# Index scores in rounds of one width, C's scores two blocks at a time, and x loaded in two column pieces

## What is computed

```python
for l in range(DEPTH):                       # DEPTH = 2
    h = _rmsnorm(x, norm_g[l])
    p = _split(h @ w_in[l])                  # 19 projections out of one
    o_a = _mla(...)                          # A: latent attention
    o_b = _diff_attn(...)                    # B: differential attention, 2 maps of 32 a head
    o_c = _dsa(p["c_q"], p["c_k"], p["c_v"], p["c_qidx"], p["c_kidx"], p["c_widx"], rel_bias, topk)
    o_d = _short_conv(...)                   # D: convolution of width 3
    y = concat([o_a * silu(p["a_gate"]), o_b * silu(...), o_c * silu(...), o_d * silu(...)])
    x = x + y @ w_out[l]
x = _rmsnorm(x, final_g)
# second_block: FFN, mixed attention, cross attention, FFN, norm
```

## Time and profile before

| | |
|---|---|
| median of 3 runs | 1757.62 us (1757.21 to 1757.74) |
| profiled execution, its own time | 1759.74 us |
| its span, first to last instruction | 1757.9 us |
| busy in the span: PE, DVE, ACT, POOL | 100%, 59%, 43%, 24% |
| chain that ended last | PE 99%, of it L1113 80% |
| weight casts L1876 on ACT (whi) | x279, 1059 ns each |
| low parts L839 on POOL (wlo) | x160, 1369 ns each |

### The profile page before, as it was taken

How to read it: one execution, slowest core, us unless ns; L and a number is a source line. 1 busy time by engine, 2 the same in 40 slices (tenths; PEclk the granted TensorE clock), 3 DMA queues, 4 the chain that set the end, 5 groups by cost and what they waited for, 6 DMA issues and landing times.

```text
span 1757.9 us, 25383 instructions
## 1 busy us (share of the span) xinstructions
PE 1749.2 (100%) x9298; PEld 1435.9 (82%) x9298; DVE 1032.4 (59%) x2170; ACT 757.8 (43%) x1396; POOL 421.5 (24%) x326
## 2 busy tenths in 40 slices
PE   9999999999999999999999999999999999999998
PEld 7778878777887888888888888889888888888887
DVE  4888776688877665555433455445756655555333
ACT  6466644546564523233233455556434322222222
POOL 4545553454644500000000332330200200000000
PEclk9999999999999999999999999999999999999999
DMA  6432123323212343333333422223322333333332
GB/s 192 129 100 73 49 65 93 96 68 105 73 49 73 103 132 96 98 96 98 102 108 103 155 61 84 85 84 109 96 73 61 91 100 97 95 95 95 102 103 94
DMA packets 54421, 166.18 MB, mean 95 GB/s; under 512 B 10200, under 2 KB 10712, under 8 KB 54328
## 3 DMA queue, kind: packets, MB, share of 16 engines
q1 hardware_dynamic: 53032, 162.12, 30.6%
q10 hardware_dynamic: 1296, 2.84, 0.5%
HBM read 162.25 MB, written 2.17 MB: 94 GB/s over the span
## 4 chain that ended last, share of the span: by engine, by line
PE 99%; DMA 0%; DVE 0%; ACT 0%; ACTq 0%; POOL 0%; issue 0%; DVEq 0%
PE proj L1113 80%; PE turned L1427 2%; PE o L1449 2%; PE proj L1591 1%; PE proj L1584 1%; PE o L1692 1%; PE o L1792 1%; PE score L1397 1%; PE turned L1079 1%; PE turned L1671 1%; PE score L1781 1%; PE proj L1301 1%; PE turned L1654 1%; PE score L1386 1%; PE score L1654 0%; PE score L1269 0%
## 5 line engine op out<-in xcount | busy, mean ns | idle before, releaser
L1113 PE MATMUL proj<-hhi,whi 128*128 128x512 f32 x1456 | 582.6, 400 | 0.0
L1113 PE MATMUL proj<-hhi,wlo 128*128 128x512 f32 x1456 | 568.4, 390 | 0.0
L1113 PE MATMUL proj<-hlo,whi 128*128 128x512 f32 x1456 | 567.4, 390 | 0.0
L1876 ACT ACTIVATE whi<-ring 128x1024 fp32r<-128x1024 f32 x279 | 295.4, 1059 | 623.7 <-PE proj L1113 602.3
L2384 DVE TENSOR_TENSOR wlo<-ring,whi 128x1024 fp32r<-128x1024 f32 x199 | 243.2, 1222 | 161.2 <-ACT whi L1876 160.7
L1113 PEld LDWEIGHTS proj<-hhi,whi 128*128 128x128 f32 x1456 | 274.0, 188 | 63.6 <-issue 10.4
L1113 PEld LDWEIGHTS proj<-hhi,wlo 128*128 128x128 f32 x1456 | 273.4, 188 | 58.6
L1113 PEld LDWEIGHTS proj<-hlo,whi 128*128 128x128 f32 x1456 | 274.1, 188 | 53.5 <-issue 0.7
L839 POOL TENSOR_TENSOR wlo<-ring,whi 128x512 fp32r<-128x512 f32 x160 | 215.5, 1369 | 339.9 <-ACT whi L1876 339.9
L857 POOL TENSOR_TENSOR prob<-prob 128x512 f32<-128x512 f32 x36 | 56.9, 1581 | 872.2 <-ACT prob L1872 872.2
L1902 ACT ACTIVATE prob<-prob,negmax 128x256 f32<-128x256 f32 (+3 forms) x208 | 114.0, 550 | 74.1 <-DVE negmax L2457 73.4
(11 more groups left out here) (379 smaller groups left out, 2436.9 us busy)
## 6 DMA issues: line engine op xcount, KB each, us to landing
ring<-wstream SPq DMA_DIRECT2D x285, 512.0 KB, 3.6
arena<-lines SPq DMA_DIRECT2D x28, 256.0 KB, 5.7
arena<-x ACTq DMA_DIRECT2D x4, 512.0 KB, 6.3
out<-arena SPq DMA_DIRECT2D x8, 256.0 KB, 2.9
arena<-mem SPq DMA_DIRECT2D x1, 1024.0 KB, 8.5
ring<-wstream SPq DMA_DIRECT2D x12, 64.0 KB, 2.2
ring<-wstream ACTq DMA_DIRECT2D x2, 256.0 KB, 7.7
arena<-rope SPq DMA_DIRECT2D x4, 128.0 KB, 6.4
```

What stands on the lines that cost most here:

```text
L1113: mm = pe.matmul(b, rounded(w), rounded(rhs(v, k)), start=(first and n == 0 and p == 0), stop=(last and n == len(blocks) - 1 and p == 2))
L1876: act.activation(rounded(dst), src, ACT.Copy, scale=scale).then_inc(ready, 1)
```

## The change

Three parts, none of which changes what is computed.

1. **Setup.** x comes in two column pieces of 512 columns, each in four transfers of 256 KB, on the queues of SyncE and ScalarE; half of the first weights stand between the pieces. The order of the column blocks is 1, 2, 3, 0, 4 to 7. TensorE issues 8 warming matmuls, the first piece's 16 transposes, 4 more small matmuls, and the first four high products, and then turns one token tile of the second piece ahead of each of the four low products. Squares are taken in halves, the second weights' rounded copy is made by GpSimd instead of ScalarE, and a copy of x moves from ScalarE to VectorE. `norm_spread` of the second job goes behind its last block.
2. **Index rounds.** `idx_unit` gives the eight units of 512 columns first, then the eight of 384, then the eight of 256. So a round has one width, and successive sums on VectorE go into the same row: a sum waits for the one just before.
3. **C.** Blocks go in the order 0, 2, 3, 1. Steps 24 and 28 issue the scores of their own 128-wide block and of the next step's 384-wide block, which share a bank (128 + 384 = 512 columns); steps 25 and 29 issue none. `attention_cost` is adapted, and `fill_plan` then gives steps 24 to 33 chunks of 4, 4, 5, 7, 4, 8, 4, 7, 5, 8 instead of 5, 3, 5, 6, 6, 6, 6, 6, 6, 7.

```diff
-WARM = 12
-X_ORDER = (1, 2, 3, 4, 5, 6, 7, 0)
+WARM = 8
+X_ORDER = (1, 2, 3, 0, 4, 5, 6, 7)
...
+C_ORDER = (0, 2, 3, 1)
 def step_qb(s):
-    return QB_ORDER[s // 2 % 4 if s < B_STEPS else s % 4]
+    return C_ORDER[s % 4] if s >= C_STEP else QB_ORDER[s // 2 % 4 if s < B_STEPS else s % 4]
...
+def double_step(s):
+    return C_STEP <= s < STEPS and s % 4 == 0
+def after_double(s):
+    return C_STEP <= s < STEPS and s % 4 == 1
...
-    elif s < 2 or B_STEPS <= s < STEPS:
+    elif double_step(s):
+        blocks += 0.25 * (step_qb(s) + 1) + 0.2 * (step_qb(s + 1) + 1)
+    elif (s < 2 or B_STEPS <= s < STEPS) and not after_double(s):
...
 def idx_unit(n):
-    return 4 * (n // (4 * (NQB - 1))) + n % 4, n % (NQB - 1) + 1
+    return n % 8, NQB - 1 - n // 8
...
         def score_bank(s, b):
+            if after_double(s):
+                return score[b][:, width(step_qb(s - 1)):S]
...
+            sp.dma_start(ident[:, :], ident_in).then_inc(ident_loaded, 16)
+            for tok in (0, 2):
+                load_x(sp, 0, tok)
+            load_w0(0, w0_loaded)
+            for tok in (0, 2):
+                load_x(sp, 1, tok)
+            load_w0(1, wload[0])
+            sp.dma_start(ring[:, 1, :], wstream[TAKE_FROM[1]]).then_inc(wload[1], 16)
...
+                for n in range(NT):
+                    high_product(n)
                 for n in range(KC + LOW_LAG):
                     if n < KC:
                         k = X_ORDER[n]
+                        if n < NT:
+                            turn_x(1, n)
+                        else:
+                            high_product(n)
                         pe.wait_ge(h_ready, n + 1)
...
-                    if k == KC - 2:
-                        pe.wait_ge(xt_out, 1)
+                    if k == KC:
+                        pe.wait_ge(xt_out2, 1)
                         norm_spread(R_NORM)
...
-                        for p, (q_part, k_part) in enumerate(((q_hi, k_hi), (q_hi, k_lo), (q_lo, k_hi))):
-                            for b in range(2):
-                                parts(b, q_part, k_part, p == 0, p == 2)
+                        for t in (s, s + 1) if double_step(s) else (s,):
+                            for p, (q_part, k_part) in enumerate(((q_hi, k_hi), (q_hi, k_lo), (q_lo, k_hi))):
+                                for b in range(2):
+                                    parts(t, b, q_part, k_part, p == 0, p == 2)
...
-            act.wait_ge(wload[1], 16)
-            act.wait_ge(hi_ready, 1)
-            make_high(1, 1)
-            act.wait_ge(h_ready, 1)
-            act.activation(xT[:, 1, :], x_bank[1][:, :], ACT.Copy).then_inc(x1_out, 1)
-            square_x(3)
+            for tok in range(NT):
+                square_x(tok, 1)
+            act.wait_ge(hi_ready, 2)
...
-                        if n < NQB - 1:
+                        if h == 0:
                             dve.tensor_scalar(index[:, qb - 1, 0:W], relu[:, n % 4, 0:W], w, None, ALU.mult).then_inc(idx_added, 1)
                         else:
-                            dve.wait_ge(idx_added, L * IDX_UNITS + (n - 2))
+                            dve.wait_ge(idx_added, L * IDX_UNITS + n)
                             dve.scalar_tensor_tensor(index[:, qb - 1, 0:W], relu[:, n % 4, 0:W], w, index[:, qb - 1, 0:W],
                                                      ALU.mult, ALU.add).then_inc(idx_added, 1)
...
-                    scores_there(L * LAYER_SM + (2 * s + 2), L * LAYER_GR + groups_before(s - 1) if s >= 2 else None)
+                    scores_there(L * LAYER_SM + (2 * s + (4 if double_step(s) else 2)), L * LAYER_GR + groups_before(s - 1) if s >= 2 else None)
```

More of the change, by code:

```diff
@@ L407, in layer_units @@
 def layer_units():
-    return [(branch, pair, qb, h, m) for branch in "BAC" for pair in range(2) for qb in QB_ORDER for h in range(2)
+    return [(branch, pair, qb, h, m) for branch in "BAC" for pair in range(2)
+            for qb in (C_ORDER if branch == "C" else QB_ORDER) for h in range(2)
             for m in range(2 if branch == "B" else 1)]
@@ L554, in build @@
         part_done = sem("part_done")
-        x_loaded = [sem(f"x_loaded{t}") for t in range(NT)]
+        x_loaded = [[sem(f"x_loaded{i}_{t}") for t in range(NT)] for i in range(2)]
+        sq_split = sem("sq_split")
         ident_loaded, gain_loaded, par_loaded = sem("ident_loaded"), sem("gain_loaded"), sem("par_loaded")
@@ L878, in _ @@
                     .then_inc((w0_lo, lo_ready)[half], 1)
+            pool.wait_ge(wload[1], 16)
+            for half in range(2):
+                cols = slice(half * SLOT // 2, (half + 1) * SLOT // 2)
+                last_copy = pool.tensor_copy(rounded(whi[:, 1, cols]), ring[:, 1, cols])
+            last_copy.then_inc(hi_ready, 1)
             pool.wait_ge(hi_ready, 2)
@@ L1064, in _, with turn_x @@
             pe.wait_ge(ident_loaded, 16)
-            for tok in range(NT):
-                pe.wait_ge(x_loaded[tok], 16)
-                for c in range(KC):
+            def turn_x(piece, tok):
+                pe.wait_ge(x_loaded[piece][tok], 16)
+                for c in range(4 * piece, 4 * piece + 4):
+                    if c == KC - 1 and tok == 0:
+                        pe.wait_ge(x0_out, 1)
                     mm = pe.transpose(x_bank[c][:, tok * P:(tok + 1) * P], xnat[:, tok, c * P:(c + 1) * P], ident[:, :])
@@ L1357, in scores @@
                 def scores(s):
-                    if 2 <= s < B_STEPS and s % 2:
+                    if 2 <= s < B_STEPS and s % 2 or after_double(s):
                         return
@@ L1390, in scores, with parts @@
                         return
-                    def parts(b, q_part, k_part, first, last):
-                        branch, pair, qb, h, m = UNITS[2 * s + b]
+                    def parts(t, b, q_part, k_part, first, last):
+                        branch, pair, qb, h, m = UNITS[2 * t + b]
                         q, W = slice(qb * P, (qb + 1) * P), width(qb)
                         rows = slice(HD * h + 32 * m, HD * h + 32 * m + 32) if branch == "B" else slice(HD * h, HD * h + HD)
-                        mm = pe.matmul(score[b][:, 0:W], rounded(q_part[rows, pair, q]), rounded(k_part[rows, pair, 0:W]),
+                        mm = pe.matmul(score_bank(t, b)[:, 0:W], rounded(q_part[rows, pair, q]), rounded(k_part[rows, pair, 0:W]),
                                        start=first, stop=last)
@@ L1960, in _ @@
                     act.wait_ge(h_ready, KC)
-                    for c in range(4, KC):
+                    for c in (6, 4, 5, 7):
                         act.activation(xT[:, c, :], x_bank[c][:, :], ACT.Copy).then_inc(xt_out2, 1)
```

72 lines of the change are left out of this document (43 added, 29 removed).

## The result

The changed kernel takes 1761.36 us (median of 11 runs, 1759.56 to 1764.99), the kernel before, on the same chip, 1757.54 (11 runs, 1756.98 to 1759.39). The ratio is 1.0018, with an interval of 1.0009 to 1.0026: slower by 3.8 us, 0.2%. Forecast were 1756.3 and a range that ended at 1758.6. The profiled execution took 1761.5, its span is 1759.7.

A forecast was written before the change was run, and what follows sets the result against it. TensorE, busy for the whole span, was taken to bound the kernel. Index rounds +0.3 (-1.92 + 2.2), C -1.16 and setup -0.5 sum to -1.36, from the median 1757.62 to 1756.3 us; 8-in-10 range 1753.6 to 1758.6.

The forecast's parts named there:

- the size of TensorE's wait in the index rounds: Last index round of each layer: TensorE waits about 1.1 us for ScalarE's fourth copy, 2.2 in two layers; bounds 0 to 1.9.
- a sign of being wrong: Index rounds: no TensorE idle time, or idle time ahead of several rounds, would show the forecast wrong.
- forecast for 56.6: VectorE's start of CKV's eviction, moved from 54.61 to about 56.6 by chained sums and wider columns, together 4.2 us less idle time.
- one more sum: Upper bound of the index wait, about 1.9 us a layer, if one more VectorE sum meets a GpSimd operation.
- so I count nothing there: One job before CKV's eviction: the fourth copy ends about level with TensorE's arrival, so no wait was counted.
- The chain's price by itself: VectorE's index sums: each chained sum costs about 0.2 us more; 14 of the first 16 are chained, 2.9 us.
- I see no new wait: C's new chunk plan: softmax is read two steps later and the shortest steps keep 2.8 us, so TensorE gets no wait.
- a forecast of 1.16: C's joined scores in steps 24 and 28: 0.29 us saved per double, four doubles, 1.16 us; bounds 1.4 saved or nothing.
- a forecast of 0.5: Setup: 0.5 us saved, the second job starting at 18.0 instead of 18.52; bounds 1.0 saved to 0.3 lost.
- The saving of the rounds: TensorE's index rounds of one width: 4.32 us a layer instead of 5.28, 0.96 saved, 1.92 in two layers.
- The slower rival: VectorE's chain of sums in CQ1 and CKV blocked by GpSimd, 1.0 us per caught sum; 1763 us; chance 0.06.
- point of decision: The slower rival decides from a wait of 3.6 us a layer, some three more caught sums per layer than counted.

The follow-up runs named there:

- e3_square_last: Changed kernel with ScalarE's square of the evicted job moved behind the fourth clamped copy of its round instead of the second: 1758.52 us, 1.0003 of the kernel before.
- e12_chain_alone: Kernel before, same units and mixed rounds, but each index sum waits for the one just before instead of three before: 1758.74 us, 1.0001 of the kernel before.
- e2_idx_only: Kernel before with only the index part of the change: 1763.67 us, 1.0028 of the kernel before.
- e4_narrow_first: Changed kernel with the narrow index rounds first (256, then 384, then 512 columns), sums still chained: 1760.1 us, 1.0010 of the kernel before.
- e5_two_rows: Changed kernel with index sums going to two rows in turn, added together behind the eighth unit: 1758.44 us, 0.9996 of the kernel before.
- e7_C_only: Kernel before with only the C part of the change: 1756.58 us, 0.9989 of the kernel before.
- e8_busy_wait: Changed kernel with 8 unread 128 x 128 matmuls on TensorE ahead of the first layer's sixth index round: 1760.83 us, 1.0014 of the kernel before.
- e10_all_mended: Changed kernel with two sum rows, the square behind the fourth copy and one more VectorE memset in setup: 1757.13 us, 0.9988 of the kernel before.
- e9_two_more: Changed kernel without its index part, plus two unread one-column memsets on VectorE at the start of setup: 1756.9 us, 0.9991 of the kernel before.

## Why the prediction was wrong

**The step that failed is the size of TensorE's wait in the index rounds**: "I take 1.1, 2.2 in two layers". It was 3.1 in the first layer and 1.7 in the second, 4.8 in all, and ahead of two rounds in each layer, which the prediction had named as a sign of being wrong. The mechanism was the forecast one: sums, eviction, square, copies, round (`e3_square_last` takes a link out, and 2.9 us of waiting go). VectorE, GpSimd and ScalarE ahead of the sixth round:

```profile
46.58 1.81 DVE L2629 SCALAR_TENSOR_TENSOR arena<-arena 128x512 f32<-128x512 f32 x1
48.31 0.68 DVE L2526 TENSOR_TENSOR arena<-proj,R 128x512 f32<-128x512 f32 x1
...
54.82 3.24 DVE L2629 SCALAR_TENSOR_TENSOR arena<-arena 128x384 f32<-128x384 f32 x2
57.98 0.68 DVE L2526 TENSOR_TENSOR arena<-proj,R 128x512 f32<-128x512 f32 x1
```
```profile
46.55 2.99 POOL L871 TENSOR_TENSOR wlo<-ring,whi 128x512 fp32r<-128x512 f32 x2 [4.91 <-ACT whi L1937]
...
54.78 2.86 POOL L871 TENSOR_TENSOR wlo<-ring,whi 128x512 fp32r<-128x512 f32 x2 [3.78 <-ACT whi L1937]
```
```profile
58.70 0.63 ACT L2050 ACTIVATE prob<-arena 128x512 f32<-128x512 f32 x1 [3.22 <-DVE arena L2526]
59.23 0.64 ACT L2068 ACTIVATE arena<-o 128x256 f32<-128x256 f32 x2
```

- *Ahead of the sixth round.* CKV's eviction was forecast for 56.6, counted from the same start of CQ1's first round. It starts at 57.98 in a stream that is 0.68 ahead of before's, so at 58.66: 4.05 later than before, where 2.0 were forecast. The last two sums take 3.24. Free they would take 0.62 + 0.10 + 0.62 = 1.34, so 1.9 is lost to GpSimd's pair, which began 0.04 ahead of them. Before, that pair caught two sums behind the eviction, where one took 1.77 and the one ahead of it 0.97 instead of 0.61; the later chain ran into it ahead of the eviction. I had this as the upper bound ("one more sum"), and it was two. Some meetings of before fell away in exchange: taking from each caught operation ahead of this eviction the length of a free one of its form, I estimate 3.7 us of blocking before and 5.3 after.
- *Ahead of the fourth round*, "so I count nothing there" was wrong. The eighth 512-wide sum began at 46.58, 0.03 behind another such pair, and took 1.81 instead of 0.75, so CQ1's eviction came 1.06 late, and 0.87 of it reached TensorE.
- *The chain's price by itself* was about right. The eviction moves by 1.8 in `e12_chain_alone`, where nothing else is changed, and sums stand 0.10 apart where they overlapped by 0.08. But it costs TensorE only 0.3 a layer there. What costs 3 in the first layer is that shift together with the wider sums and the new meetings, on a TensorE that comes earlier; how the 3 divides among them no run shows.

**"I see no new wait" was right for C and wrong for setup**, where the text looked for none outside the setup. C gave 1.1 alone and 1.1 in the change, for a forecast of 1.16. Setup gave 0.4 for a forecast of 0.5, and took back 0.93 near 146, through a pause of VectorE that it moved and the same blocking by GpSimd. The lock of the Trainium skill (Trainium Architecture — The Big Picture, What this means for kernel authors) holds both ways there, and the traces agree: VectorE's operation takes 1.79 instead of 0.85 where it starts 0.04 later than GpSimd's, and GpSimd's 1.74 instead of 1.28 where that starts 0.26 later.

**The saving of the rounds**, 1.92, was right. With the two wrong terms replaced the forecast's own sum is -1.36 + (4.8 - 2.2) + 0.93 = +2.2 us, at the lower end of what runs of like clock show (2.1 to 2.8).

**The rest up to 3.8 is the clock.** After's profile has a fall to 1.2 GHz at 61, before's one at 198, each worth 1.6, and how often either kernel has one decides its median. The prediction took before's profile to be 2.1 above its median without asking why. Whether the waits make such a fall more frequent is open: by their times, five of after's 11 runs were free of it, and eight of before's 11 beside them. The falls with no wait near have one thing in common. TensorE's timeline of before ahead of its fall, and the window of the fall:

```profile
194.79 1.84 PE L1079 MATMUL proj<-halves,tmp 128*128 128x2 f32 x16
```
```profile
198.00:201.30 3.30, 3.30 (x20) 2.68 (x17) 3.16 (x14) 1.22 (x5) 3.30 (x4) 0.50 0.02 6
```

These 16 matmuls of two columns, which add up squares of B's outputs, stand once in each layer. In the 14 profiles eight falls begin 2.7 to 3.4 us behind the first of them, five in the first layer and three in the second; in the other 20 passes the clock stays at 2.4 GHz. So the place is known, and what decides there is not.

**The slower rival** named the right mechanism and the right place. Its point of decision, 3.6 us of wait a layer, was not reached (3.1 and 1.7). The kernel got slower all the same: the wait beyond the forecast, 2.6, is more than the 1.36 that the forecast had to gain, and the setup's wait and the clock, which the rival didn't count, came on top.

## What to carry to other kernels

When a change makes one engine later, write down which operations of the other engine on the same memory it will newly meet, and count each meeting at full length, since the one that has to wait does so until the other is through; where the starts are some 0.05 us apart, don't count on being first. When parts of a change are timed together, each part is worth a run alone: here the chain of sums took away what the rounds of one width gave, setup moved a wait to another place, and the parts that held beat both kernels together. And before a change of 0.2% is judged, see what the clock did in the runs of either kernel, and compare like with like.

## What the runs showed of the hardware

- The clock of TensorE falls to 1.2 GHz for a few us, at a price of 1.6, at the same places in some executions and not in others: at 61, behind a wait of 2.2 (the change, `e2_idx_only`, but not `e4_narrow_first` behind 2.3), or behind the 16 matmuls of two columns with no wait near, at 197 to 204 (before, `e2_idx_only`, `e3_square_last`, `e5_two_rows`, `e7_C_only`) and at 495 to 505 (`e2_idx_only`, `e8_busy_wait`, `e10_all_mended`). One more fall, at 1749 in `e3_square_last`, stands behind 16 matmuls of one column. What decides whether it falls stays open.
- VectorE pauses for 0.34 us at one place of its stream, which the number of instructions ahead of it moves. In a stretch where VectorE waits anyway it costs nothing (`e9_two_more`); just ahead of a meeting with GpSimd it decided who came first.
- A sum of 384 or 512 columns that meets GpSimd in SBUF takes 1.45 to 1.8 instead of 0.62 to 0.86 (the product of two tiles at L2704 included). An eviction out of PSUM beside the same GpSimd operation kept its 0.68 (48.31, with L871 running from 46.55 to 49.54).
